# Three unread f32 products of 256 columns on TensorE, and VectorE's modulation pieces placed inside its two waits for ScalarE

## The reference

```python
def ada_modulation(c, ada_w, ada_b):          # ada_w is 1024 x 6144, one c vector
    m = jax.nn.silu(c) @ ada_w + ada_b
    return jnp.split(m, 6, axis=-1)

def even_layer(x, c, ...):                    # odd_layer: the same frame, with attention
    sh_m, sc_m, g_m, sh_f, sc_f, g_f = ada_modulation(c, ada_w, ada_b)
    h = modulate(rms_norm(x, mix_norm), sh_m, sc_m)
    ...                                       # mixer
    x = x + g_m * y
    hf = modulate(rms_norm(x, ffn_norm), sh_f, sc_f)
    return x + g_f * ((silu(hf @ ffn_w_gate) * (hf @ ffn_w_up)) @ ffn_w_down)
```

## Time and profile before

| | |
|---|---|
| median of 3 runs | 1174.51 us (1173.94 to 1174.69) |
| the profiled execution | 1177.91 us, of it span 1176.3 us |
| TensorE busy | 1161.4 us, 99% of the span |
| VectorE busy | 882.2 us, 75% |
| ScalarE busy | 633.7 us, 54% |
| granted TensorE clock | 1.00 over the whole span |
| DMA | 248.96 MB, mean 212 GB/s |

### The profile page before, as it was taken

The page is one execution under the profiler, slowest core; times in us unless marked ns, Lnnn a source line. Parts: engine busy times, 40 slices in busy tenths (PEclk is TensorE's granted clock), DMA queues, the critical chain, the costliest instruction groups (busy, mean ns, idle before and its releaser), DMA issues.

```text
span 1176.3 us, 22917 instructions
## 1 busy us (share of the span) xinstructions
PE 1161.4 (99%) x9553; PEld 1124.4 (96%) x9553; DVE 882.2 (75%) x1177; ACT 633.7 (54%) x853; POOL 98.4 (8%) x147
## 2 busy tenths in 40 slices
PE   8999999999999999999999999999999999999998
PEld 8999999999998999999999999999988779999998
DVE  5876778878766778778889887887777657866543
ACT  6657566633447576633558554343556665543432
POOL 0000001110034001011100001111000000000000
PEclk9999999999999999999999999999999999999999
DMA  8452568887662577787653658868846505576362
GB/s 312 156 179 72 180 220 281 303 309 247 233 233 73 180 252 256 278 317 282 234 181 129 192 159 298 277 233 297 274 147 246 181 5 188 184 262 212 120 198 84
DMA packets 150060, 248.96 MB, mean 212 GB/s; under 512 B 5554, under 2 KB 80923, under 8 KB 149979
## 3 DMA queue, kind: packets, MB, share of 16 engines
q1 hardware_dynamic: 135858, 197.17, 49.8%
q0 software_dynamic: 13952, 50.60, 11.7%
q10 hardware_dynamic: 168, 0.04, 0.0%
HBM read 246.74 MB, written 1.05 MB: 211 GB/s over the span
## 4 chain that ended last, share of the span: by engine, by line
PE 85%; DVE 5%; issue 1%; ACT 1%; DMA 1%; POOL 0%; DVEq 0%; POOLq 0%
PE ps L2153 25%; PE ps L2155 25%; PE ps L2154 25%; DVE w_lo L1262 3%; PE ps L2439 2%; DVE scratch L1764 1%; PE ps L2305 1%; PE ps L2755 1%; ACT w_hi L747 1%; PE ps L2421 1%; DMA ada_raw<-in_l_ada_w 1%; PE ps L2729 1%; PE ps L2408 1%; PE ps L2771 1%; PE ps L2238 0%
## 5 line engine op out<-in xcount | busy, mean ns | idle before, releaser
L1262 DVE TENSOR_TENSOR w_lo<-raw,w_hi 128x2048 fp32r<-128x2048 f32 (+4 forms) x196 | 412.9, 2145 | 94.3 <-ACT w_hi L747 94.0
L747 ACT ACTIVATE w_hi<-raw 128x2048 fp32r<-128x2048 f32 (+4 forms) x196 | 342.1, 1791 | 159.4 <-PE ps L2155 148.8
L2153 PE MATMUL ps<-h_both,w_hi 128*128 128x256 f32 (+1 forms) x1296 | 361.6, 279 | 2.8 <-DVE w_lo L1262 2.1
L2155 PE MATMUL ps<-h_both,w_lo 128*128 128x256 f32 (+1 forms) x1296 | 359.7, 278 | 0.0
L2154 PE MATMUL ps<-h_both,w_hi 128*128 128x256 f32 (+1 forms) x1296 | 359.7, 278 | 0.0
L2153 PEld LDWEIGHTS ps<-h_both,w_hi 128*128 128x128 f32 (+1 forms) x1296 | 242.8, 187 | 4.2 <-issue 3.4
L2155 PEld LDWEIGHTS ps<-h_both,w_lo 128*128 128x128 f32 (+1 forms) x1296 | 244.0, 188 | 0.0
L2154 PEld LDWEIGHTS ps<-h_both,w_hi 128*128 128x128 f32 (+1 forms) x1296 | 242.9, 187 | 0.1
L2153 PE MATMUL ps<-a_both,w_hi 128*128 128x256 f32 x864 | 239.1, 277 | 0.0
L2155 PE MATMUL ps<-a_both,w_lo 128*128 128x256 f32 x864 | 238.6, 276 | 0.0
L2154 PE MATMUL ps<-a_both,w_hi 128*128 128x256 f32 x864 | 238.6, 276 | 0.0
(11 more groups left out here) (425 smaller groups left out, 1814.6 us busy)
## 6 DMA issues: line engine op xcount, KB each, us to landing
ada_raw<-in_l_ada_w POOLq DMA_DIRECT2D x96, 512.0 KB, 7.0
raw<-in_mlp_w_up SPq DMA_DIRECT2D x32, 1024.0 KB, 6.6
raw<-in_mlp_w_down SPq DMA_DIRECT2D x32, 1024.0 KB, 6.4
raw<-in_l_ffn_w_gate SPq DMA_DIRECT2D x22, 1024.0 KB, 5.5
raw<-in_l_ffn_w_up SPq DMA_DIRECT2D x22, 1024.0 KB, 9.2
raw<-in_l_ffn_w_down SPq DMA_DIRECT2D x16, 768.0 KB, 5.7
raw<-in_l_w_qkv SPq DMA_DIRECT2D x12, 1024.0 KB, 6.7
raw<-in_l_w_in SPq DMA_DIRECT2D x10, 1024.0 KB, 6.3
```

The costliest lines, as they stand in the source:

```text
L747: nc.scalar.activation(w_hi[:, s.slot, cut], raw[:, s.slot, cut], ACT.Copy).then_inc(split_hi, 1)
L1262: nc.vector.tensor_tensor(w_lo[:, s.slot, cut], raw[:, s.slot, cut], w_hi[:, s.slot, cut].bitcast(F32), ALU.subtract).then_inc(split_lo, 1)
L2153: nc.tensor.matmul(to, sh, mh, start=first, stop=False, skip_group_check=True)
L2155: return nc.tensor.matmul(to, sl, mh, start=False, stop=last, skip_group_check=True)
```

## The change

Two things. **First**, TensorE's unread product of 128 columns at the third slot of each `gate_up` goes, and three unread f32 products of 256 columns of `scratch` with `ones` come: one in the first slot of `w_o0`, after the first quarter of its 96 products, and one between the two banks of slot 2 of `gate_up0` and of `gate_up1`. **Second**, in `hidden(j)` VectorE does the first half unit after the multiplication (while ScalarE copies the high part) and the second half unit after the low part (while ScalarE makes `w_hi`). In `gate_up0` the slot's second unit comes after the `w_lo` of slot j+2. The number of units per slot is as before.

```diff
-            def ada_unit(m):
+            def ada_half(m, q):
                 slot, quarter = m % 2, m % 4
                 dve.wait_ge(ada_loaded[slot], 16 * (m // 2 + 1))
...
+            def ada_halves(n):
+                for at in range(halves_begun[0], halves_begun[0] + n):
+                    ada_half(at // 2, at % 2)
+                    if at % 8 == 7:
+                        ada_group_done(at // 8)
+                halves_begun[0] += n
             def ada_units(n):
+                ada_halves(2 * n)
...
@@ hidden(j) @@
-                    if j < 10 or l == 0:
-                        ada_units(2 - l)
+                    halves = 1 if j < 10 or l == 0 else 0
                     dve.wait_ge(parts_done, s.before + 2)
                     dve.wait_ge(acc_out[0], turn(f"gate_up{l}", j) + 1)
                     nc.vector.tensor_tensor(full, full, two(1), ALU.mult).then_inc(acc_out[1], 1)
+                    ada_halves(halves)
                     dve.wait_ge(hid_hi, HIDDEN_BEFORE[f"ffn{l}"] + j + 1)
                     nc.vector.tensor_tensor(a_lo[:, at_pair, :], full, a_hi[:, at_pair, :].bitcast(F32),
                                             ALU.subtract).then_inc(hid_lo, 1)
+                    ada_halves(halves)
                     split(ahead)
+                    if l == 0:
+                        ada_units(1)
@@ TensorE @@
+            def unread_product():
+                nc.tensor.matmul(ps[:, NORM_BANK, 0:T], ones[:, :], scratch[:, 0, :], start=True, stop=True, skip_group_check=True)
-            as_chunks_arrive("w_o0", 0, hi=o_hi, lo=o_lo)
+            as_chunks_arrive("w_o0", 0, hi=o_hi, lo=o_lo, sums_after=0, sums=unread_product)
...
-                pe.wait_ge(split_lo, Slot(f"gate_up{l}", 2).split + 2)
-                wait_acc(0, turn(f"gate_up{l}", 2))
-                nc.tensor.matmul(ps[:, NORM_BANK, 0:P], ones[:, :], ident[:, :], start=True, stop=True, skip_group_check=True)
-                for j in (2, 3):
-                    two_bank_slot(f"gate_up{l}", j)
+                two_bank_slot(f"gate_up{l}", 2, between=unread_product)
+                two_bank_slot(f"gate_up{l}", 3)
```

More of the change, by code:

```diff
@@ L1752, in _ @@
             ada_sum = scratch[:, 2:4, :].rearrange("p c t -> p (c t)")
-            def ada_unit(m):
+            def ada_half(m, q):
                 slot, quarter = m % 2, m % 4
                 dve.wait_ge(ada_loaded[slot], 16 * (m // 2 + 1))
[L1758 to L1767, removed]
-            def ada_units(n):
[L1771 to L1775, removed]
+                w, c = ada_raw[:, slot, q, :], silu_c[:, 2 * quarter + q:2 * quarter + q + 1]
+                if quarter == 0 and q == 0:
+                    ins = nc.vector.tensor_scalar(ada_sum, w, c, None, ALU.mult)
+                else:
+                    dve.wait_ge(ada_step, m * 2 + q)
+                    ins = nc.vector.scalar_tensor_tensor(ada_sum, w, c, ada_sum, ALU.mult, ALU.add)
+                ins.then_inc(ada_step, 1)
+            halves_begun = [0]
+            def ada_halves(n):
[4 more added lines that the diff above has]
+                halves_begun[0] += n
+            def ada_units(n):
+                ada_halves(2 * n)
             def ada_group_done(g):
@@ L2215, in ada_combine, with two_bank_slot @@
                 ins.then_inc(ada_combined, 1)
-            def two_bank_slot(phase, j, i=None, step=0, hi=h_hi, lo=h_lo, apart=0):
+            def unread_product():
+                nc.tensor.matmul(ps[:, NORM_BANK, 0:T], ones[:, :], scratch[:, 0, :], start=True, stop=True, skip_group_check=True)
+            def two_bank_slot(phase, j, i=None, step=0, hi=h_hi, lo=h_lo, apart=0, between=None):
                 s = Slot(phase, j, i, step)
@@ L2222, in two_bank_slot @@
                 for b in range(2):
+                    if b and between:
+                        between()
                     wait_acc(b, turn(phase, j, i, step) - apart)
```

## The result

The changed kernel is slower: 1185.4 us as the median of 9 runs (1181.2 to 1193.9) against 1176.3 for the kernel before (9 runs, 1173.9 to 1180.6), a ratio of 1.0082, with a 95% interval of 1.0058 to 1.0106. The profiled execution took 1189.57 us with a span of 1188.0; before it was 1177.91 with 1176.3. TensorE is busy 98% of the span, where it was 99.

The account below looks back on a forecast made before the run. TensorE, busy 99% of the span, was taken to bound the kernel. Terms -1.1 - 3.4 + 2.4 + 1.2 = -0.9 us on 1174.5 gave 1173.6 us; range 1169.6 to 1178.0, the forecast's own 1171.5 to 1176.5.

Parts of the forecast that it names:

- The stand and its mechanism: Before the third slot of `ffn_down0`: unit 79's late load holds VectorE, and TensorE idles some 5.6 us.
- Rival A: In `ffn_down0`: the load for unit 79 doesn't bind, the slots' gain stays, -7.7 us, 1166.8; chance 0.12 with in-between cases.
- The clock: Behind TensorE's idle in `ffn_down0`: the clock may fall to half speed, costing 1.2 us, ends 0 and 2.7.
- the unread products bring the fast pace: The new 256-column products turn slow to fast: -1.1 us in `w_o0`, -3.4 in `gate_up1`; none needed in `gate_up0`.
- doesn't flip: The pace stays slow behind a new product in `w_o0` (1175.2 us) or `gate_up1` (1177.2); chance 0.17.
- Rival C: Slot 2 of `gate_up0`: the new product takes away the fast pace, 3.6 us more, 1177.2; chance 0.11.
- B: The pace doesn't flip in one place: `w_o0` alone gives 1175.2 us, `gate_up1` alone 1177.2; chance 0.17.
- The slots of `gate_up0`: Nine slots of `gate_up0`: VectorE's new order removes TensorE's idle; -3.2 us with the products' cost counted.
- Rival D: `ffn_down0` restarts slow (1.8 us), and `w_o1` and `up1` turn slow (1.7): 1175.4 to 1177.1; chance 0.15.
- The restart behind the stand: After TensorE's idle in `ffn_down0`, its 396 products might run slow, costing 1.8 us.
- My one line for stand and slots: `gate_up0` and the idle in `ffn_down0` together: the slots' gain is given back and more, +2.4 us.

Follow-up runs that it names:

- no_stand: The changed kernel with unit 79 moved behind the first addition at the start of `ffn_down0`; ratio 0.9987 to the kernel before.
- early_unit: The changed kernel with the second unit of slot 10 of `gate_up0` (unit 77) ahead of the `w_lo` pair; ratio 1.0011 to the kernel before.
- vec_only: The changed kernel with TensorE's products of before, so VectorE's new order alone; ratio 1.0055 to the kernel before.
- filled_stand: The changed kernel with thirteen unread 256-column products behind TensorE's second slot of `ffn_down0`; ratio 1.0048 to the kernel before.
- prod_only: The changed kernel with VectorE's order of before, so the three 256-column products alone; ratio 0.9999 to the kernel before.

## Why the prediction was wrong

I forecast 1173.6 us and the measurement gave 1185.4. Point by point:

- *The stand and its mechanism: right, a little small.* Unit 77 behind the `w_lo`, the load for 79 issued late, VectorE's wait ended by the DMA of `ada_raw`, TensorE idle 5.94 us where I had 5.6. The load took 7.04 us, I took 6.0, which is the difference between my 20.7 us and the 21.65 measured. no_stand and early_unit confirm it from both sides. Rival A is out.
- *The clock: right in kind, too small in size.* I took 1.2 us between ends 0 and 2.7; it was 2.45 in the trace (2.2 in vec_only), and filled_stand, in which TensorE rested 0.98 us instead of 5.94, lost none of it. My sentence that the clock of before is at its upper level over the whole span is wrong at its start, by my own: the first twelve products took 244 ns each, half speed, though the profile writes 1.00 there. The mean granted clock was 0.995 to 0.998 in all 19 runs of the two kernels with the stand, and 0.999 or 1.000 in every run of the others. The Trainium skill, "TensorE: Matmul & The Clock Gate", Part 1 on the clock gate, by which the sum would have been the high end, is borne out: the granted clock was down at 814 and up again at 820 (25 products in 5.35 us between).
- *The step that failed: the unread products bring the fast pace.* I had -1.1 in `w_o0` and -3.4 in `gate_up1`, and nothing lost in `gate_up0`. In the trace after, `w_o0` was fast from its first product, ahead of the new one; `gate_up1` was slow and stayed so; `gate_up0` was fast up to slot 3 and slow from there. In the 14 `gate_up` phases with the product inside slot 2 ten started slow, and one of them became fast. I had taken the turn at one product for its effect, against the earlier trace rows, and given "doesn't flip" 0.17 where it was the rule. Rival C saw the loss in `gate_up0` and B that in `gate_up1`, each alone; they came together.
- *The slots of `gate_up0`: right, on a condition that I did not name.* 3.2 us were forecast; 2.8 came in vec_only, where the pace was fast, and 0.7 is all there is where it is slow.
- *Rival D*: the throw in `w_o1` and `up1` came out slow, +1.7, in this execution; vec_only and prod_only, in which no edit touches `w_o1` either, had it fast. The restart behind the stand, D's other half, came out fast.
- *The sum.* With the stage terms alone (stand +5.95, clock +2.45, less 2.8 in the slots, plus 0.4, 0.2 and 0.2 for the products) the changed kernel is 6.4 us over before. In vec_only the stages of its own trace give 5.8 (`ffn_down0` +8.65, slots -2.85), and it measured +0.55%, 6.5 us. The medians before and after lie 9.1 us apart; I put the 2.7 us above the 6.4 down to pace, which the trace shows (`gate_up0` slow from slot 3, `w_o1` and `up1`, `ffn_down1`), but a trace is one execution and can't say it of the median. My one line for stand and slots (+2.4) should have been some +3.3 at the fast pace. So of the 10.0 us between the change that I forecast (-0.9) and the measured one (+9.1), 5.1 are the products in `w_o0` and `gate_up1` (-4.5 forecast, +0.6 spent), some 1.2 the clock and 0.9 stand and slots; the last 2.7 are pace, as far as is known.
- *The range.* I gave the pace rivals as single throws on one kernel time. One kernel's runs lie 10 to 15 us apart by the pace, so 1174.5 as the time of before was itself a draw of three (other chips gave medians up to 1179.7), and "0.2% can be told apart" was too fine.

## What to carry to other kernels

When a piece is moved behind the step that frees a buffer, follow the buffer and not the engine: the load that it delays comes back as a wait several steps later, and if it makes TensorE rest for long (5.9 us here, but not 0.6 or 1.0) it is paid twice, in the rest and in the clock. A pace that differs between two executions of the same code need not be an effect of the instruction that happens to stand at the change; look at a second trace of the same kernel before building on it. And the gain from taking away an engine's waits should be worked out at each pace that the other engine can have.

## What the runs showed of the hardware

- Two paces of TensorE at the same granted clock of 1.00, 113.3 and 117.8 ns for a product of 256 columns, each kept over hundreds of products. The same kernel shows either in the same phase in different executions. In 20 traces, from `w_o0` on, no single f32 product of 256 columns inside or between slots was followed by the slow pace out of the fast one (37 places), and out of the slow one it was followed by the fast one in 9 of 27. At the column sum near 44 us it is otherwise: the pace was fast ahead of it in 13 of the 20 traces and slow behind it in all 20, among them. There the weights and the other operand change sides at the product, and no run separates the two. So the product alone fixes the pace in neither direction. Eight transposes were followed by the slow one in each of the four places where they were put.
- In the rest of 5.9 us the granted clock fell to 0.50, and it stayed there through the 25 products behind (22 in vec_only, after 6.5 us). With products in the same gap, and only 0.98 us of rest, it stayed at 1.00.
- Loads of `ada_raw` (512 KB) landed in 4.0 to 7.5 us in the 50 us around this one place, and for the load of unit 79 the difference of 7.0 and 4.3 us is worth 2.6 us of stand.
